# Down stage of a four-layer fp32 network: first weight sums by an adding DMA from GpSimd, and the instruction order around the stage

## What is computed

```
def conv_ffn(x, w_up, conv_w, conv_b, w_down):
    h = x @ w_up                                  # 1024 -> 2 * 2816
    h = depthwise conv of width 3 over tokens + conv_b
    gate, val = jnp.split(h, 2, axis=-1)
    return (jax.nn.silu(gate) * val) @ w_down     # 2816 -> 1024
...
    x = x + rms_norm(m, post_mix)
    x = x + rms_norm(conv_ffn(rms_norm(x, pre_ffn), *ffns[i]), post_ffn)
```

## Time and profile before

| what | value |
|---|---|
| median of 3 runs | 2090.82 us (2089.89 to 2091.44) |
| the profiled execution, its own time | 2094.57 us |
| its span, first to last instruction | 2092.8 us |
| PE busy | 2062.1 us |
| DVE busy | 1420.1 us |
| ACT busy | 1024.3 us |
| POOL busy | 335.3 us |
| mean granted clock of PE | 0.995 |
| loads `raw<-slabs` | 368, of 512 KB |
| DMA, mean over the span | 112 GB/s |

### The profile page before, as it was taken

The page is one execution under the profiler, slowest core; times in us unless marked ns, Lnnn a source line. Parts: engine busy times, 40 slices in busy tenths (PEclk is TensorE's granted clock), DMA queues, the critical chain, the costliest instruction groups (busy, mean ns, idle before and its releaser), DMA issues.

```text
span 2092.8 us, 32448 instructions
## 1 busy us (share of the span) xinstructions
PE 2062.1 (99%) x11724; PEld 1729.9 (83%) x11724; DVE 1420.1 (68%) x2282; ACT 1024.3 (49%) x1671; POOL 335.3 (16%) x390
## 2 busy tenths in 40 slices
PE   9999999999999999999999999999999999999998
PEld 8889888778988888877877898888788889888776
DVE  6665555799366555599888665556997665555797
ACT  4754333457335433446656553334565764333455
POOL 1520212100000121100045402112000520211100
PEclk9999999999999999999999999999999999999999
DMA  7123332254431332245421123223454132322353
GB/s 284 62 101 122 100 100 91 93 177 151 142 128 54 101 100 94 86 141 177 165 71 41 62 69 112 91 90 100 141 176 157 62 102 71 100 91 90 101 181 111
DMA packets 66713, 234.84 MB, mean 112 GB/s; under 512 B 7424, under 2 KB 11648, under 8 KB 66224
## 3 DMA queue, kind: packets, MB, share of 16 engines
q1 hardware_dynamic: 58752, 213.10, 30.4%
q10 hardware_dynamic: 7856, 20.34, 2.8%
HBM read 231.26 MB, written 6.34 MB: 114 GB/s over the span
## 4 chain that ended last, share of the span: by engine, by line
PE 87%; DVE 7%; DMA 3%; issue 1%; ACT 1%; SPq 0%; POOL 0%; DVEq 0%; ACTq 0%; POOLq 0%
PE ps L1964 15%; PE ps L1965 15%; PE ps L1966 15%; PE ps L2149 6%; PE ps L2483 6%; PE ps L2485 6%; PE ps L2484 6%; DMA raw<-slabs 3%; PE ps L2036 2%; DVE work L1710 2%; PE ps L1992 2%; PE ps L1994 2%; PE ps L1993 2%; PE ps L2024 1%; PE ps L2008 1%; PE ps L2009 1%
## 5 line engine op out<-in xcount | busy, mean ns | idle before, releaser
L1964 PE MATMUL ps<-h_hi,w_hi 128*128 128x512 f32 (+1 forms) x1552 | 606.6, 391 | 0.0
L1965 PE MATMUL ps<-h_lo,w_hi 128*128 128x512 f32 (+1 forms) x1552 | 603.2, 389 | 0.0
L1966 PE MATMUL ps<-h_hi,w_lo 128*128 128x512 f32 (+1 forms) x1552 | 603.2, 389 | 0.0
L1710 DVE SCALAR_TENSOR_TENSOR work<-ps,conv_sb,work 128x511 f32<-128x511 f32 (+1 forms) x352 | 246.2, 744 | 379.5 <-ACT work L1108 379.3
L1315 DVE TENSOR_TENSOR w_lo<-raw,w_hi 128x1024 fp32r<-128x1024 f32 x356 | 439.8, 1241 | 43.0 <-ACT w_hi L747 41.5
L747 ACT ACTIVATE w_hi<-raw 128x1024 fp32r<-128x1024 f32 x368 | 384.2, 1051 | 140.1 <-DVE raw L1788 79.5
L1108 ACT ACTIVATE work<-ps,conv_sb 128x512 f32<-128x512 f32 x176 | 137.1, 779 | 490.8 <-PE ps L1966 461.3
L1964 PEld LDWEIGHTS ps<-h_hi,w_hi 128*128 128x128 f32 x1552 | 291.4, 188 | 62.9 <-issue 4.0
L1966 PEld LDWEIGHTS ps<-h_hi,w_lo 128*128 128x128 f32 x1552 | 291.3, 188 | 60.4
L1965 PEld LDWEIGHTS ps<-h_lo,w_hi 128*128 128x128 f32 x1552 | 291.5, 188 | 58.4
L698 POOL TENSOR_TENSOR bias<-act 128x256 f32<-128x256 f32 x40 | 67.5, 1687 | 997.8 <-DVE act L1716 997.8
(11 more groups left out here) (273 smaller groups left out, 3215.6 us busy)
## 6 DMA issues: line engine op xcount, KB each, us to landing
raw<-slabs SPq DMA_DIRECT2D x368, 512.0 KB, 3.3
bias<-slabs SPq DMA_DIRECT2D x16, 512.0 KB, 5.9
act<-slabs SPq DMA_DIRECT2D x12, 512.0 KB, 5.9
...
g_post<-gains ACTq DMA_DIRECT2D x8, 512.0 KB, 4.2
...
g_pre<-gains ACTq DMA_DIRECT2D x7, 512.0 KB, 5.2
x<-x_in SPq DMA_DIRECT2D x4, 512.0 KB, 7.3
```

The costliest lines, as they stand in the source:

```text
L1710: ve.scalar_tensor_tensor(y, ps[:, 2 * par + e, 0:SEQ - sh], conv_sb[:, L, t, tap:tap + 1], y, ALU.mult, ALU.add).then_inc(done, 1)
L1964: pe.matmul(ps[:, bank, cols], hi, h_hi[:, k, cols], start=k == 0, stop=False)
L1965: pe.matmul(ps[:, bank, cols], hi, h_lo[:, k, cols], start=False, stop=False)
L1966: last = pe.matmul(ps[:, bank, cols], lo, h_hi[:, k, cols], start=False, stop=k == KT - 1)
```

## The change

It does six things.

1. **T1 by DMA.** From step 3 on (`T1_DMA = 3`), DVE makes no T1. POOL issues two DMAs per step in `first_sums`: B11 from DRAM to the place of T1, and, once that has landed, B12 from DRAM added onto it. Each moves 128 rows of 2 KB (256 KB). Each pair starts when the low part of the step's operand is made (`op_lo`), since T1's place is in that operand's space. ACT's `t1(j)` then waits for `t1_in`.
2. **Signs.** A DMA can add, so T1 = B11 + B12 with no minus: the scheme's signs are turned. The even slabs' B11 and product 1 are as they were in size and number; `u3`, `c12` and `c22` subtract where they added. The host's slabs are not changed in shape or order. The number and shape of these instructions stays.
3. **Early operands.** The high parts of operands 1 and 2 go to `g_post` and `g_pre`, the low parts over the activations themselves, so that `operand(1)` and `operand(2)` can be made before PE has left `h_hi` and `h_lo`. Operands from 3 on use the ring of four in `h_hi` and `h_lo`.
4. **Gains later.** `load_gains(2L+2)` moves from before the up stage into ACT's step 3 of the down stage, behind a wait for `w_used` of 6 slabs, since the two buffers hold operands until then.
5. **Order at the end of the up stage.** ACT and DVE make the sums, `s1` and splits earlier; on DVE the low parts of slabs 0 and 1 stand ahead of the taps of pair 20, not behind them.
6. **Order at the norms.** ACT does `second(5)` before `root_post(1)`; where the next layer is not the sparse one, `split_early(n + 3)` moves behind `root_pre(2)` on ACT and behind `norm(2)` on DVE.

```diff
+        EARLY_OPS = 3
+        T1_DMA = 3
...
             if j == 0:
                 return a_hi[:, :, :], a_lo[:, :, :]
-            q = 2 * ((j - 1) % 4)
+            if j < EARLY_OPS:
+                return two((g_post_r, g_pre_r)[j - 1][:, :]), act_r[:, 2 * j:2 * j + 2, :]
+            q = 2 * ((j - EARLY_OPS) % 4)
             return h_hi[:, q:q + 2, :], h_lo[:, q:q + 2, :]
...
+            def first_sums(L):
+
+                for j in range(T1_DMA, STEPS):
+                    even = slabs[dram(DOWN[L] + 2 * j)]
+                    pool.wait_ge(op_lo, STEPS * L + j + 1)
+                    pool.dma_start(t1_place(j), even[:, 0:SEQ]).then_inc(t1_first, 16)
+                    pool.wait_ge(t1_first, t1_count(L, j))
+                    pool.dma_start(t1_place(j), even[:, SEQ:D], accum_op=ALU.add).then_inc(t1_in, 16)
...
                 down_sums(L)
+                first_sums(L)
...
                 operand(L, 0)
-                s1(L, 0)
-                s1(L, 1)
+                for j in range(4):
+                    s1(L, j)
+                operand(L, 1)
                 pair(1, end - 1)
-                s1(L, 2)
-                s1(L, 3)
-                pair(0, end)
                 s1(L, 4)
                 s1(L, 5)
+                operand(L, 2)
+                s1(L, 6)
+                s1(L, 7)
+                tap(0, end, 0)
+                split_hi(DOWN[L])
+                tap(0, end, 1)
+                split_hi(DOWN[L] + 1)
+                silu(0, end)
                 tap(1, end, 0)
                 split_hi(DOWN[L] + 2)
-                s1(L, 6)
-                s1(L, 7)
                 tap(1, end, 1)
-                operand(L, 1)
                 split_hi(DOWN[L] + 3)
+                operand(L, 3)
                 silu(1, end)
...
-                    sc.wait_ge(t_made, 4 * (STEPS * L + j) + 1)
+                    if j < T1_DMA:
+                        sc.wait_ge(t_made, t_count(L, j, 1))
+                    else:
+                        sc.wait_ge(t1_in, t1_count(L, j))
...
                     split_hi(n0 + 2 * j)
                     split_hi(n0 + 2 * j + 1)
+                    if j == 3:
+                        sc.wait_ge(w_used, n0 + 2 * EARLY_OPS)
+                        load_gains(k)
...
                 root_pre(0)
+                second(5)
                 root_post(1)
-                second(5)
                 second(6)
...
                     root_post(3)
+                    root_pre(2)
                     split_early(n + 3)
-                    root_pre(2)
...
-                load_gains(2 * L + 2)
...
-                ve.tensor_tensor(b12, b11, t3, ALU.subtract).then_inc(t_made, 1)
+                ve.tensor_tensor(b12, t3, b11, ALU.subtract).then_inc(t_made, 1)
...
                     split_lo(n0 + 2 * j - 2)
-                    sums(L, j)
+                    odd_sum(L, j)
                     split_lo(n0 + 2 * j - 1)
```

More of the change, by code:

```diff
@@ L182, in build @@
         t_made = sem("t_made")
+        t1_first = sem("t1_first")
+        t1_in = sem("t1_in")
         op_hi = sem("op_hi")
@@ L377, in t1_place, with t_count, t1_count @@
             return act[:, {0: 22, 1: 23, 2: 1}.get(j, 2 * j), :]
+        EARLY_OPS = 3
+        T1_DMA = 3
+        def t_count(L, j, n):
+            steps = STEPS * L + j
+            return 3 * steps + T1_DMA * L + min(j, T1_DMA) + (n if j < T1_DMA else n - 1)
+        def t1_count(L, j):
+            return 16 * ((STEPS - T1_DMA) * L + j - T1_DMA + 1)
         def op_parts(j):
@@ L1734, in ffn_up @@
                 s1(L, 1)
-                sums(L, 0)
+                first_sum(L, 0)
+                s1(L, 2)
+                s1(L, 3)
+                operand(L, 1)
+                odd_sum(L, 0)
                 next_sum(L, 0)
@@ L1738, in ffn_up @@
                 pair(1, end - 1)
-                s1(L, 2)
-                sums(L, 1)
-                s1(L, 3)
-                next_sum(L, 1)
-                last_sum(L, 1)
-                pair(0, end)
                 s1(L, 4)
                 s1(L, 5)
-                split_lo(DOWN[L] + 2)
+                operand(L, 2)
+                first_sum(L, 1)
                 s1(L, 6)
-                sums(L, 2)
                 s1(L, 7)
+                split_lo(DOWN[L])
+                odd_sum(L, 1)
+                next_sum(L, 1)
+                split_lo(DOWN[L] + 1)
+                last_sum(L, 1)
+                taps(0, end)
+                first_sum(L, 2)
+                gate(0, end)
+                odd_sum(L, 2)
                 next_sum(L, 2)
                 last_sum(L, 2)
+                split_lo(DOWN[L] + 2)
                 taps(1, end)
-                operand(L, 1)
                 split_lo(DOWN[L] + 3)
@@ L1768, in operand, with first_sum, odd_sum @@
                 ve.tensor_tensor(lo, act[:, 2 * j:2 * j + 2, :], hi.bitcast(f32), ALU.subtract).then_inc(op_lo, 1)
[L1770 to L1778 removed]
+            def first_sum(L, j):
+                even = DOWN[L] + 2 * j
+                b11, b12 = raw[:, raw_slot(even), 0:SEQ], raw[:, raw_slot(even), SEQ:D]
+                ve.wait_ge(raw_in[raw_slot(even)], raw_count(even))
+                if j == 2:
+                    ve.wait_ge(op_lo, STEPS * L + 1)
+                ve.tensor_tensor(t1_place(j), b12, b11, ALU.add).then_inc(t_made, 1)
+            def odd_sum(L, j):
+                even, odd = DOWN[L] + 2 * j, DOWN[L] + 2 * j + 1
+                b12, b22 = raw[:, raw_slot(even), SEQ:D], raw[:, raw_slot(odd), SEQ:D]
                 ve.wait_ge(raw_in[raw_slot(odd)], raw_count(odd))
[L1780 removed]
+                ve.tensor_tensor(b22, b22, b12, ALU.subtract).then_inc(t_made, 1)
             def next_sum(L, j):
@@ L1822, in third @@
                     ve.wait_ge(d_made, 2 * L + i + 1)
-                    ve.tensor_tensor(u3_place(i), ps[:, 2 * i + 1, :], d_place(i), ALU.add).then_inc(u3_made, 1)
+                    ve.tensor_tensor(u3_place(i), d_place(i), ps[:, 2 * i + 1, :], ALU.subtract).then_inc(u3_made, 1)
                 def c21(i):
@@ L1833, in c12 @@
                     ve.wait_ge(m_done, (TT - 1) * (k - 1) + i + 1)
-                    ve.tensor_tensor(ps[:, 5 + 2 * i, :], ps[:, 2 * i + 1, :], p1_place(i), ALU.add).then_inc(c12_made, 1)
+                    ve.tensor_tensor(ps[:, 5 + 2 * i, :], ps[:, 2 * i + 1, :], p1_place(i), ALU.subtract).then_inc(c12_made, 1)
                 def c22(i):
```

37 lines of the change are left out of this document (16 added, 21 removed).

## The result

The changed kernel takes 2107.68 us (median of five runs, 2104.46 to 2118.04) against 2090.82 before (five runs, 2089.89 to 2091.44): 1.0094 times the time before, 95% interval 1.0081 to 1.0108. It is slower by 17 us, and the forecast was 2075. The profiled execution took 2111.04 us with a span of 2109.3, 16.5 us more than the span of before.

The account below looks back on a forecast made before the run. PE was taken as the bound, busy 2062 of 2092.8 us, its excess waits giving 25.5 us to gain. 25.5 - 10 + 2.3 - 2.0 = 15.8 us saved gave a forecast of 2075 us, range 2063 to 2090.

Parts of the forecast that it names:

- signs that it named: Trace signs listed beforehand: right, DVE's step at 5.2 to 5.7 us; wrong, step loads over 4.4 us, among others.
- Wait for the taps: End of the up stage: PE's long wait for the taps of pair 21 goes, 11.3 us gained.
- the clock behind it: After the tap wait: the slower clock that follows PE's standing goes too, 6.6 us gained.
- the step's third term: Down-stage steps: DVE's pace, 5.81 us a step against PE's 5.44, makes PE wait at 20 boundaries, 7.6 us.
- Third transposes: Norms of layers 0 and 2: PE's 1.23 us wait shrinks to about 0.2, 2.3 us gained.
- second(5): Norms: the root comes 0.95 us later; PE waits 0.9 more in layer 0, about 0.5 in layers 1 and 2: 2.0 lost.
- T1 off DVE: Down-stage steps: without T1 DVE needs 5.22 us a step, under PE's 5.44, so 7.6 us are gained.
- The new DMAs: Down-stage steps 4 to 10: GpSimd's pairs lengthen slab loads, 2.5 us lost a layer, 10 us in all.
- x: Lengthening of a 3.2 us slab load in the steps; bounds 0 and 1.1 us, taken as 0.6.
- the formula: DVE's step is 5.14 + x us, slower than PE's 5.44 above x = 0.3.
- the raw load becomes the bound: Rival, 12%: pairs and slab loads land in turn, loads take 3.2 + 1.7 us, DVE's step 6.84, total 2106 us.
- The gains: Before step 4: gain loads and a later operand 5 leave some 0.6 us lead; 1 us a layer added for refills and crowd.

Follow-up runs that it names:

- e3: Changed kernel with T1 made by DVE in all steps and gains loaded after the steps, the new order kept: 2073.2 us, 0.9914 of the kernel before.
- e9: e2 with both low parts of the step before moved ahead of T3 in DVE's order: 2073.9 us, 0.9921 of the kernel before.
- e10: e9 with second(5) put back behind root_post(1) on ACT: 2067.8 us, 0.9890 of the kernel before.
- e6: e3 with second(5) put back behind root_post(1) on ACT: 2071.6 us, 0.9909 of the kernel before.
- e1: Changed kernel with T1 made by DVE in all steps, gains still loaded at step 3: 2081.9 us, 0.9958 of the kernel before.
- e2: Changed kernel with GpSimd's DMA pairs kept and gains loaded after the steps: 2101.9 us, 1.0055 times the kernel before.
- e5: e2 with only the first, plain copy of each DMA pair, so T1 lacks a term: 2074.9 us, 0.9930 of the kernel before.
- e7: e3 with GpSimd's DMA pairs also running, one DMA at a time, into an unread scratch buffer: 2102.1 us, 1.0052 times the kernel before.
- e11: e2 with both DMAs of each pair cut to half their columns, 128 KB each: 2087.7 us, 0.9983 of the kernel before.

## Why the prediction was wrong

Of the signs that it named, these came: no long wait for the taps, clock 1.00 in the windows, 0.1 us at the third transposes, and no wait for T1. DVE's step did not stay between 5.2 and 5.7 us, and of the signs of being wrong came loads of over 4.4 us in the steps.

*Wait for the taps, 11.3 us, and the clock behind it, 6.6.* Right: 10.7 became 0.9, and the window at 405 shows 1.00. The window at 905 and the one at 1473 do too. The layout by hand put the taps at 402.9 to 405.6; they ran from 402.46 to 405.17. The order alone measured 17.0 us of gain for 18.2 worked out. That is closer than it deserves, since some of the 17.0 belongs to the step's third term (below).

*Third transposes, 2.3 us.* Right. In layers 0 and 2 PE waits 0.10 us where it waited 1.23, 2.3 us less. The 2.8 us that the view after still lists are 2.1 in layer 1, which has the other branch, and 0.7 at the start of the kernel.

*second(5), 2.0 us lost.* Right in sign; 1.6 measured on e3, 6.1 on e9. The place was not: a wait of over 1.2 us was to stand in layer 0, and in the changed kernel it sits in three layers (idle 0.5, 0.65 and 0.5 us), in layer 0 shorter than the 1.2 of before.

*T1 off DVE, 7.6 us.* Too much. Where the loads are covered in both, e10 against e6, it is 3.8 us; e9 against e3 shows nothing (+0.7). The better start of the steps already gives much of what I had booked to T1: by its start times PE waits for a low part, mostly some 0.1 us, at 18 boundaries of steps before, and at 9 in e3, where DVE still makes every T1.

*The new DMAs, 10 us.* This is the step that failed, in its size. With T1's 7.6 it made the move to DMA a net loss of 2.4 us; the runs show 25.8 (against e1) and 28.7 (e2 against e3). The step said itself "there is no slack", 3.4 against 3.48, and set the price by x. I took x = 0.6 "since the data of a pair are under way for about half of each step". That did not even follow from my own lower bound, 2 x 2.1 = 4.2 us of 5.44. A pair is under way all the time: a copy took 4.0 us at the median and not 2.1, nor the 2.6 of the estimate beside it (3.2 for the lone copy in e5), and an adding one took 5.4; each copy is issued while the adding DMA before it is under way.

x came out at 1.3 as the median of all slabs in the window, and about 1.5 for the odd slab of the step shown, for which 4.93 us lie between place and T3. With 1.5 the formula gives a step of 6.64; the trace has 6.67 there. Put into the prediction's sum, x = 1.5 gives 8.8 us a layer, 35 in all, and a time of 2100; most of what is missing to 2107.7 is T1's 7.6, of which at most 3.8 were there, and the gains.

The rival "the raw load becomes the bound", 12%, said loads of 3.2 + 1.7 = 4.9 us, a step of 6.84 and 2106. It had the mechanism and the load: the odd slabs took 5.0 on average, and the kernel 2107.7. That the total fits to 2 us is in part luck, since the steps were longer (7.25) and the 7.6 of T1 stood in its sum as well. The bounds of x, 0 and 1.1, came from the earlier trace rows, that is from slabs beside slabs, and the case lay above both. Here a DMA of GpSimd is open beside two loads; that this third transfer is the reason is a reading that fits e5, e7 and e11, and no more.

*The gains, inside the 1 us a layer that was added for refills and their crowd.* Too small. With 0.6 us of lead left, a slab of 8.2 us cannot be covered: 3.3 to 3.6 us of standing in three layers, and the slower clock behind each. They cost 5.8 us in all where the pairs run and 8.6 where DVE makes T1, not 4 or less.

*The method.* The formula was right in form, and its answer turned from gain to loss between x = 0.6 and 1.2, a span that no row could narrow. There the bad side deserved more than 12%: a step without slack pays for each lengthening in full, and receives nothing for a shortening. And the cover of 3.48 us was itself a matter of one row's place in DVE's order, which I had read and not questioned.
